# The triangular inversion of a chunked recurrence on its 32x32 diagonal blocks

## The reference, cut to what matters

```python
def step(state, inp):
    r_t, w_t, k_t, v_t, kk_t, b_t = inp
    sk = jnp.einsum('bhvk,bhk->bhv', state, kk_t)
    state = (state * w_t[:, :, None, :] - sk[..., None] * b_t[:, :, None, :]
             + v_t[..., None] * k_t[:, :, None, :])
    return state, jnp.einsum('bhvk,bhk->bhv', state, r_t)
```

## Time and profile before

| what | value |
|---|---|
| median of 3 runs | 2197.64 us (2195.75 to 2203.24) |
| the profiled execution, device time | 2195.71 us |
| its span in the trace | 2194.4 us |
| around the span (2195.71 less 2194.4) | 1.3 us |
| PE busy, share of the span | 97% |
| PEld, DVE, ACT | 85%, 67%, 45% |
| granted clock of PE, mean | 0.992 |

### The profile page before, as it was taken

The page is one execution under the profiler, slowest core; times in us unless marked ns, Lnnn a source line. Parts: engine busy times, 40 slices in busy tenths (PEclk is TensorE's granted clock), DMA queues, the critical chain, the costliest instruction groups (busy, mean ns, idle before and its releaser), DMA issues.

```text
span 2194.4 us, 45350 instructions
## 1 busy us (share of the span) xinstructions
PE 2125.9 (97%) x19810; PEld 1869.3 (85%) x19810; DVE 1463.6 (67%) x2479; ACT 994.8 (45%) x1735; POOL 133.1 (6%) x124
## 2 busy tenths in 40 slices
PE   8999999999999989879999999999999999999999
PEld 3877788888778878768889999999988899999987
DVE  5889888887796855965577676334666657766622
ACT  4225655655625343335454444323666654443311
POOL 0000000000000004233410000000000030000000
PEclk9999999999999999999999999999999999999999
DMA  7631011111332533100133223224210023222322
GB/s 292 129 112 50 22 70 46 46 46 46 126 105 87 166 123 108 42 11 20 35 118 96 85 89 95 87 84 141 69 39 30 22 85 107 87 94 90 89 99 72
DMA packets 60021, 184.26 MB, mean 84 GB/s; under 512 B 7184, under 2 KB 11280, under 8 KB 59824
## 3 DMA queue, kind: packets, MB, share of 16 engines
q1 hardware_dynamic: 59824, 181.37, 26.1%
HBM read 174.73 MB, written 6.62 MB: 83 GB/s over the span
## 4 chain that ended last, share of the span: by engine, by line
PE 84%; DVE 9%; ACT 3%; issue 1%; DMA 1%; POOL 0%; SPq 0%; DVEq 0%
PE PS L603 67%; PE PS L788 3%; PE PS L777 2%; DVE ca L2062 2%; PE PS L1148 2%; PE PS L1279 2%; PE PS L797 1%; PE PS L1247 1%; DVE wlo L1960 1%; ACT Lb L1327 1%; DVE Swk L2496 1%; DVE mx L2492 1%; PE PS L1121 1%; PE PS L768 1%; DMA early<-in_wall 1%
## 5 line engine op out<-in xcount | busy, mean ns | idle before, releaser
L603 PE MATMUL PS<-nhi,whi 128*128 128x264 f32 (+1 forms) x2064 | 431.3, 290 | 2.4 <-ACT Vk L1327 1.5
L603 PE MATMUL PS<-nhi,wlo 128*128 128x264 f32 (+1 forms) x2064 | 418.1, 284 | 1.5 <-DVE wlo L1960 1.5
L603 PE MATMUL PS<-nlo,whi 128*128 128x264 f32 (+1 forms) x2064 | 418.6, 284 | 0.0
L1327 ACT ACTIVATE whi<-raw 128x1024 fp32r<-128x1024 f32 (+3 forms) x322 | 306.6, 953 | 199.5 <-PE PS L603 199.5
L1960 DVE TENSOR_TENSOR wlo<-raw,whi 128x1024 fp32r<-128x1024 f32 (+1 forms) x257 | 307.8, 1205 | 88.9 <-ACT whi L1327 88.8
L603 PEld LDWEIGHTS PS<-nhi,whi 128*128 128x128 f32 x2064 | 321.4, 190 | 9.7 <-ACT Vk L1327 1.7
L603 PEld LDWEIGHTS PS<-nhi,wlo 128*128 128x128 f32 x2064 | 320.8, 189 | 1.8 <-DVE wlo L1960 1.7
L603 PEld LDWEIGHTS PS<-nlo,whi 128*128 128x128 f32 x2064 | 321.3, 189 | 0.0
L603 PE MATMUL PS<-hhi,whi 128*128 128x512 f32 x648 | 266.2, 411 | 0.6 <-DVE hlo L2015 0.4
L603 PE MATMUL PS<-hhi,wlo 128*128 128x512 f32 x648 | 256.6, 396 | 7.0 <-DVE wlo L1960 6.9
L603 PE MATMUL PS<-hlo,whi 128*128 128x512 f32 x648 | 254.9, 393 | 0.0
(11 more groups left out here) (390 smaller groups left out, 3479.8 us busy)
## 6 DMA issues: line engine op xcount, KB each, us to landing
raw<-in_wall SPq DMA_DIRECT2D x266, 512.0 KB, 3.6
early<-in_wall SPq DMA_DIRECT2D x16, 512.0 KB, 14.7
raw<-in_wall SPq DMA_DIRECT2D x16, 384.0 KB, 3.1
TZ<-g_rows SPq DMA_DIRECT2D x2, 2112.0 KB, 9.0
raw<-in_wall SPq DMA_DIRECT2D x32, 128.0 KB, 2.0
raw<-in_wall SPq DMA_DIRECT2D x16, 256.0 KB, 2.6
g_rows<-gsb SPq DMA_DIRECT2D x8, 328.0 KB
xt<-in_xT SPq DMA_DIRECT2D x2, 1024.0 KB, 8.5
```

The lines of the kernel that those rows point to most:

```text
L603: q = e.matmul(out, cuts[a][:, k * P:(k + 1) * P], (hi_, lo_)[b][:, kr, lo:lo + w], start=start and k == 0 and a == b == 0, stop=stop and ...
L1327: return e.activation(out, src, func, **kw)
```

## The change

Levels 1 to 4 of the inversion, and level 0, work only on the 32x32 diagonal blocks of a 64x64 matrix: each of the matmuls of 64x64 by 64 columns becomes two of 32x32 by 32 columns, on the two blocks (`crossing_blocks`, `beside_blocks`, 32 matmuls where there were 16). The operands `To`, `X`, `XT` and `Wb` are kept as 32 columns, so that DVE and ACT handle 128x256 elements instead of 128x512. The last level computes one 32x32 block for each matrix (16 matmuls instead of 16 of 64x64), and `XTf` holds the full inverse, put together by DVE in pieces of 32 partitions.

The square of T is split. `blocks()` makes first, into the banks 2 and 3, what the inversion needs: 32 matmuls with 32 columns of weights and 64 or 32 columns streamed. `square_late()` makes the other 64 columns, 16 matmuls. DVE takes the first mask directly out of the banks; ACT copies the rest of them to `Td`. The order string `PERIOD` is unchanged. `blocks()` takes the banks 2 and 3, and so waits for their last readers.

```diff
+                def crossing_blocks(bb, lhs, rhs, first=(0, 1), second=(0, 1)):
+                    for h in range(2):
+                        for t in range(4):
+                            for half, rows in enumerate(rowsof):
+                                to_half = half ^ (t % 2)
+                                g, to = place(rows, t, h), place(rowsof[to_half], t, h) // 2
+                                for q, r in zip(first, second):
+                                    m = e.matmul(PS[block_rows(to_half, r), bb[half], to * 32:to * 32 + 32], lhs(block_rows(half, q), g),
+                                                 rhs(block_rows(half, q), g), start=True, stop=True)
...
+                def beside_blocks(b, lhs, rhs, first=(0, 1), second=(0, 1)):
+                    for g in range(8):
+                        for half in range(2):
+                            for q, r in zip(first, second):
+                                m = e.matmul(PS[block_rows(half, r), b, g * 32:g * 32 + 32], lhs(block_rows(half, q), g),
+                                             rhs(block_rows(half, q), g), start=True, stop=True)
...
+                def blocks():
+                    for h in range(2):
+                        for step in free[2 + h]:
+                            on.wait_ge(*at(*step))
+                        free[2 + h] = [("To_first", j), ("Td", j)]
+                    for t in range(4):
+                        for par in range(2):
+                            for h in range(2):
+                                for q in range(2):
+                                    c, g = (2 * t + par) * 64 + 32 * q, t ^ par
+                                    m = e.matmul(PS[block_rows(par, q), 2 + h, g * 64:g * 64 + 64 - 32 * q], Bf[rowsof[h], c:c + 32],
+                                                 ar[rowsof[h], t, 0, par * 64 + 32 * q:par * 64 + 64], start=True, stop=True)
...
-                square(Bf, "Tt")
+                blocks()
+                square_late()
                 yield
...
-                for lev in range(1, 6):
+                for lev in range(1, 5):
...
-                        crossing(bb, lambda rows, g: XT[rows, g, :], lambda rows, g: Wb[rows, g, :]).then_inc(*up("X_sum", j, lev))
-                    beside(b2, lambda rows, g: Wb[rows, g, :], lambda rows, g: XT[rows, g, :]).then_inc(*up("XT_sum", j, lev))
+                    crossing_blocks(bb, lambda rows, g: XT[rows, g, :],
+                                    lambda rows, g: Wb[rows, g, :]).then_inc(*up("X_sum", j, lev))
+                    beside_blocks(b2, lambda rows, g: Wb[rows, g, :],
+                                  lambda rows, g: XT[rows, g, :]).then_inc(*up("XT_sum", j, lev))
...
+                crossing_blocks(bb, lambda rows, g: Td[rows, g, 32:64], lambda rows, g: X[rows, g, :],
+                                (0,), (1,)).then_inc(*up("W_sum", j, 5))
...
+                beside_blocks(b2, lambda rows, g: Wb[rows, g, :], lambda rows, g: XTf[rows, g, 32:64],
+                              (1,), (0,)).then_inc(*up("XT_sum", j, 5))
...
+                on.wait_ge(*at("To_first", j))
+                act(Td.rearrange("p (h g) n -> p h (g n)", h=2), PS[:, 2:4, 0:256], ACT.Copy).then_inc(*up("Td", j))
...
+                        for q in (1, 0):
+                            for half in range(2):
+                                rows = block_rows(half, q)
+                                m = e.tensor_tensor(XTf[rows, :, 32 * q:32 * q + 32], XT[rows, :, :], made[rows], ALU.subtract)
```

More of the change, by code:

```diff
@@ L153 @@
     "tile": "q_tile",
-    "pair_sums": "lora_w lora_a kk_sum square turned bonus MV_sum To_turned To_crossed W_sum X_sum XT_sum PQ_sum "
+    "pair_sums": "lora_w lora_a kk_sum blocks square turned bonus MV_sum To_turned To_crossed W_sum X_sum XT_sum PQ_sum "
                  "Rp_sum KV_sum O_sum oc_sum gn_sum",
@@ L808, in steps_r, with steps_b @@
                     return lambda rows, t, h: src[rows, place(rows, t, h), 1, :]
+                def steps_b(rows, t, h):
+                    return Tt[rows, place(rows, t, h), :]
+                def crossing_blocks(bb, lhs, rhs, first=(0, 1), second=(0, 1)):
[7 more added lines that the diff above has]
+                                                 rhs(block_rows(half, q), g), start=True, stop=True)
+                    return m
@@ new lines, in square_late @@
+                def square_late():
+                    bb = pair_of(("Tt", j), ("Tt", j))
+                    for t in range(4):
+                        for par in range(2):
+                            for h in range(2):
+                                c, g = (2 * t + par) * 64, t ^ par
+                                q = e.matmul(PS[rowsof[par], bb[h], g * 64:g * 64 + 64], Bf[rowsof[h], c:c + 64],
+                                             ar[rowsof[h], t, 1, par * 64:par * 64 + 64], start=True, stop=True)
+                    q.then_inc(*up("square", "Tt", j))
@@ L822, in core @@
                 on.wait_ge(*at("To_first", j))
-                beside(b, lambda rows, g: To[0][rows, g, :], lambda rows, g: eye2[rows, :]).then_inc(*up("To_turned", j))
+                beside_blocks(b, lambda rows, g: To[0][rows, g, :], lambda rows, g: eye32[rows, :]).then_inc(*up("To_turned", j))
                 bb = pair_of(("To", j), ("XT", j, 0))
-                crossing(bb, lambda rows, g: eye2[rows, :], lambda rows, g: To[0][rows, g, :]).then_inc(*up("To_crossed", j))
+                crossing_blocks(bb, lambda rows, g: eye32[rows, :], lambda rows, g: To[0][rows, g, :]).then_inc(*up("To_crossed", j))
                 yield
@@ L836, in core @@
                     on.wait_ge(*at("X", j, lev - 1))
-                    crossing(bb, lambda rows, g: To[lev % 2][rows, g, :], lambda rows, g: X[rows, g, :]).then_inc(*up("W_sum", j, lev))
+                    crossing_blocks(bb, lambda rows, g: To[lev % 2][rows, g, :],
+                                    lambda rows, g: X[rows, g, :]).then_inc(*up("W_sum", j, lev))
                     yield
@@ L1496, in core @@
                     on.wait_ge(*at("W_sum", j, lev))
-                    act(by_bank(Wb), crossed_banks([banks["W", j, lev, r] for r in range(2)]), ACT.Copy).then_inc(*up("W", j, lev))
+                    act(by_bank(Wb), crossed_blocks([banks["W", j, lev, r] for r in range(2)]), ACT.Copy).then_inc(*up("W", j, lev))
                     yield
@@ L2087, in vector @@
             for n in range(2):
+                e.memset(XTf[block_rows(n, 1), :, 0:32], 0.0)
                 q = e.memset(zs[n][:, 0:1], 0.0)
@@ L2986, in shape_constants @@
     c[:, CBLK:CBLK + P] = same
[L2987 removed]
+    a, b = s % 32, t[:, 0:32]
+    c[:, CLEV + 160:CLEV + 192] = a == b
+    for lev in range(5):
         n = 1 << lev
[L2989 to L2990 removed]
+        c[:, CLEV + 32 * lev:CLEV + 32 * (lev + 1)] = (a // (2 * n) == b // (2 * n)) & (a // n % 2 == 0) & (b // n % 2 == 1)
     c[:, CEYE2:CEYE2 + 64] = (s % 64) == np.arange(64)[None, :]
```

99 lines of the change are left out of this document (64 added, 35 removed).

## The result

| | before | changed |
|---|---|---|
| median | 2197.09 us (2195.75 to 2203.24, 4 runs) | 2288.98 us (2283.25 to 2291.56, 4 runs) |
| ratio | 1 | 1.0406 (95%: 1.0386 to 1.0425) |
| profiled execution, span in the trace | 2194.4 us | 2288.4 us |
| start of the last group of `side` of pair 7, the end of the recurrence | 577.8 us | 667.2 us |

All times here are medians of the executions in the fast state; one of the four of `e5_burst`, at 5221 us, was not in it and is left out.

The account below looks back on a forecast made before the run. The prediction took PE's own work to bound the recurrence, with instruction supply as a second limit. Its terms, -14 + 12 + 58 = +56 us, gave 2252 us on the profiled execution, stated as 2254 us, range 2220 to 2298.

Parts of the forecast that it names:

- array work: Small matmuls and split square on PE: -1.75 us for a pair, -14 us in all, bounds -25 to +30.
- wait before `blocks`: PE waits until ACT has read banks 2 and 3: 1.4 us in six pairs, 3.7 in pair 0, +12 us.
- stops for instructions: PE runs out of instructions in the inversion's dense groups: 7.6 us for a pair, +58 us, bounds +14 to +98.
- clock: Half clock behind PE's stops in the recurrence: nothing in the sum, only a rival at +14 to +28 us, chance 0.08.
- `Td`, `XTf`: New waits for ACT's copy at level 1 and DVE's pieces in level 4: hidden, put at 0, bounds 0 to +4.
- What bounds the kernel: In the recurrence PE is busy 375.1 of 378.0 us, so less DVE and ACT work by itself gains nothing.
- the column stream sets the pace: Small matmuls on PE: about 0.11 us for 64 columns in a quarter, 0.06 us for 32 in a tile.
- small records have a floor: Rival for small matmuls: 32 columns cost a record what 64 do; +75 us in all, 2272 us, chance 0.14.
- the bound of +30: Upper bound for the small matmuls: all nine crossings 0.4 us longer, `beside` unchanged.
- the 2 us for the stretch ahead of it: PE's instruction stops before X of level 2 (186.00 to 201.42 us in the earlier trace): 2 us for a pair.
- Rival 3: Clock falls in PE's stops in the dense stretch: one or two falls for a pair, 2275 us, chance 0.08.
- Signs given in advance: Profile signs: 188 packets, 3.5 us apart in the dense stretch, mid-group "issue" stops, group times, 1.4 us before L855.

Follow-up runs that it names:

- e5_burst: The kernel before with one burst of 512 matmuls of 32x32 by 32 columns on constants put ahead of the recurrence: 2226.92 us, 1.0151.
- e2_split: The kernel before with each crossing and beside matmul of the inversion issued as two of 32 columns, still on 64x64 tiles: 2293.88 us, 1.0427.
- e12_wait_only: The kernel before with only one wait added: PE waits for `aa` of the next pair before the square of T: 2213.64 us, 1.0074.
- e10_one_pass: The changed kernel with the operands of levels 1 to 4 in bfloat16, one load and one matmul each: 2209.54 us, 1.0048.
- e6_filled: The changed kernel with three useless large matmuls ahead of each of six steps of the inversion: 2281.86 us, 1.0389.
- e9_banks: The changed kernel with the two halves of the split square exchanged in their PSUM banks: 2279.27 us, 1.0374.

## Why the prediction was right in direction, and 35 us short

| step | predicted | measured |
|---|---|---|
| array work | -14 | -5 |
| wait before `blocks` | +12 | +13 |
| stops for instructions | +58 | +45 |
| clock | 0 (rival, +14 to +28) | +35 |
| `Td`, `XTf` | 0 | 0 |
| sum | +56 | +89 (unrounded) |

The direction came from the right mechanism. That the sum came within 35 us is partly luck: the stops were put 13 us too high, which hid a part of what the clock and the array work added.

- **What bounds the kernel.** Right: shorter work of DVE and ACT brought nothing, and DVE's busy share fell from 67% to 63%.
- **Array work.** The failed step is that the column stream sets the pace. For `crossing_blocks` I wrote 0.47 us "nothing won": it is 0.56 us, 64 records 8.9 ns apart, and W and X together became 0.24 us dearer for a pair, where 0.2 was to be saved. `beside_blocks` is 0.57, not 0.5 us; XT and level 0 give 1.9 us, not 2.3. The square in two parts is 0.5 us dearer, not 0.15; the steps with other tiles around the inversion 0.5, near the 0.6 put down. In all -0.6 us for a pair in place of -1.75. That is the rival "small records have a floor" in a mild form: the bound of +30 was far too high, the value -14 too low by 9. On a 64x64 tile `e2_split` shows such a floor (28.8 ns for a record of 32 columns in `beside`, 28.5 for one of 64 before), but on 32x32 tiles the records lie 8.9 ns apart and the whole `beside` group is shorter.
- **The wait.** Right to 1 us in size; `e12_wait_only` shows it alone, 16.5 us with the clock that it costs. Its cause was half right: it is mostly what ACT has to do first, and only to a small part the two matmuls before.
- **Stops.** The mechanism is shown by the borders, the packets and the burst (128 matmuls and 128 loads from stop to stop in `e5_burst`); 188 packets came. From X of level 2 on the stops take 4.7 to 8.0 us for a pair, 5.7 in the mean, against 5.6 foreseen. The step that was mis-sized is the 2 us for the stretch ahead of it: 0.2 us in the mean, 1.1 at most (pair 2). The prediction's own working is off there, since it speaks of 3.5 us without instructions and takes off 4.1; with 3.5 it would be 1.4 us. At borders that follow each other PE goes on 3.5 to 4.0 us apart, in the burst 3.7 to 4.0, so 3.5 is the lower end of what came; what makes the difference is not shown.
- **The clock.** Rival 3 happened on top of the forecast rather than instead of it. It stood as "one or two falls for a pair", with a chance of 0.08 and the argument that small groups wait anyway. The step that failed is the pricing, a term put at nothing: with stops of 0.4 to 2.8 us PE was at 0.50 for 20 us in a row, and there k-steps, `across` and the 128-column groups pay in full: for a pair +2.2 us in the k-steps and +2.2 in the rest. The earlier trace rows had shown just such a stretch. A forecast that has such stops come several times for a pair had to carry it in the sum.
- **Signs given in advance.** 3.5 to 4 us between packets, "issue" at distances of 256, 1.4 us by `aa` at L855: seen (3.5 to 4 between packets, 1.5 to 1.6 at L855). `beside_blocks` takes 0.75 us and `crossing_blocks` 0.74 in the rows above, against 0.7 and 0.65 to 0.7. The stretch behind the recurrence was to keep its length; it grew by 4.6 us, which is not explained, and which is less than the 7 to 8 us by which the executions of one kernel differ in the table of the result.

In `e12_wait_only` the work became 0.3 us dearer for a pair by the same count, some 2 us in six pairs. So the waits by themselves bring a small part of the clock's 35 us; most of it stands behind the stops, or behind both together, which no run separates. What stays open besides is what decides after which stop the clock falls, and why the eight-tile group is held to 8.9 ns a record in float32 when the same group in bfloat16 starts 32 records in 0.12 us (`e10_one_pass`).

## What to carry to other kernels

Count instructions as well as columns: a change that splits matmuls has to be held against the rate at which instructions come (here 256 in 3.5 to 4.0 us), locally and not on the average of a stage. Where a forecast has an engine stand still several times for 2 us, price the half clock that follows on the large matmuls around it (here 0.50 for 20 us behind the first stops of pair 0, and 0.43 us from one matmul of 512 columns to the next in place of 0.23). And try the part of a change that adds no instructions by itself before the whole is written.

## What the runs showed of the hardware that I had not expected

- With no instructions in reserve PE got 256 of them in 3.7 to 4.0 us (14.5 to 15.6 ns each), and used them up in 1.3 us (`e5_burst`); in the changed kernel borders came 3.5 to 4.0 us apart.
- In float32 a matmul record on a 64x64 tile costs the same with 32 as with 64 columns: 28.8 against 28.5 ns in `beside`, 14.9 against 15.4 in `crossing`. Thirty-two columns pay only on 32x32 tiles, at 8.9 ns a record on four tiles and on eight.
- From the last record on 32x32 tiles to the first on 64x64 it is 0.12 us, the other way 0.15 us (`e6_filled`, clock at 0.99; at the half clock of the changed kernel L831 to L806 takes 0.17 and L806 to L840 0.24), from L788 to L797 on 64x64 tiles before 0.04 us.
- Added array work of 41 us made the program no longer (7 us shorter by the medians, `e6_filled`).
- A wait can hide stops: with the wait for `aa` cut from 12.8 to 6.7 us, "issue" grew from 37.5 to 46.6 us (`e9_banks`).
- The half clock comes just as well from one wait of 3.8 us in a program without any 32x32 tile (`e12_wait_only`, 0.50 in 183.1 to 187.0 us), while 12.6 us of stops of at most 1.3 us each in a dense program left it at 1.00 (`e2_split`).
